# The inverse of 128x128 triangular matrices on four quarters of the array, with sides that alternate

## The reference, cut

```python
def _rwkv7_step(S, inp):
    r, w, k, v, a, b = inp
    sa = jnp.einsum('bhvk,bhk->bhv', S, a)
    S = S * w[:, :, None, :] + sa[..., None] * b[:, :, None, :] + v[..., None] * k[:, :, None, :]
    y = jnp.einsum('bhvk,bhk->bhv', S, r)
    return S, y
...
    xs = tuple(jnp.moveaxis(u, 1, 0) for u in (r_h, w_h, k_h, v_h, -kk, kk * i_h))
    s_new, y = lax.scan(_rwkv7_step, s0.astype(jnp.float32), xs)
```

## Time and profile before

| what | value |
|---|---|
| time, median of 3 runs | 4197.47 us (4194.5 to 4198.24) |
| the profiled execution | 4201.06 us, span 4198.9 us, mean granted clock 0.979 |
| PE busy | 4016.0 us, 96% |
| DVE busy | 2009.9 us, 48% |
| ACT busy | 1386.4 us, 33% |
| chain that ended last | PE 86%, DVE 7%, ACT 2%, issue 2%, DMA 2% |
| pair stage, layer 0 | about 119 to 1153 us |
| pair stage, layer 1 | about 2164 to 3252 us |

### The profile page before, as it was taken

One profiled execution on the slowest core, in us unless ns is written; L12 is line 12 of the kernel. 1 busy time (PEld: TensorE's weight loads), 2 busy tenths in 40 slices (PEclk: granted clock), 3 DMA queues, 4 the chain that ended last, 5 costly groups with the idle time before them and its releaser, 6 DMA issues.

```text
span 4198.9 us, 84192 instructions
## 1 busy us (share of the span) xinstructions
PE 4016.0 (96%) x36004; PEld 3557.1 (85%) x36004; DVE 2009.9 (48%) x3207; ACT 1386.4 (33%) x2169; POOL 288.5 (7%) x463
## 2 busy tenths in 40 slices
PE   7999999999999998999989999999999999989998
PEld 6888888988876687999978888989888766879997
DVE  4545554544345545333355455455443555554444
ACT  4333333333322323222243333343333223232222
POOL 1000000000111021000000000000001110100000
PEclk8999999999999999999999999999999999999998
DMA  6222221222455574443332222212224555412222
GB/s 201 65 63 66 71 72 61 67 68 72 136 201 192 175 231 124 123 134 103 120 108 68 60 69 70 69 62 68 65 77 136 190 194 184 152 48 71 71 76 70
DMA packets 476463, 446.08 MB, mean 106 GB/s; under 512 B 18767, under 2 KB 408969, under 8 KB 475217
## 3 DMA queue, kind: packets, MB, share of 16 engines
q1 hardware_dynamic: 417136, 251.74, 19.8%
q0 software_dynamic: 41568, 155.70, 11.5%
q10 hardware_dynamic: 17408, 33.56, 2.2%
HBM read 344.48 MB, written 96.45 MB: 105 GB/s over the span
## 4 chain that ended last, share of the span: by engine, by line
PE 86%; DVE 7%; ACT 2%; issue 2%; DMA 2%; DVEq 0%; ACTq 0%; SPq 0%; POOL 0%
PE ps L773 84%; DVE scr L2023 4%; PE ps L777 3%; ACT scr L1464 1%; DVE w_lo L2036 1%; DVE h_lo L2023 1%; DMA scr<-in_ada_w_dram 1%; DVE lw L2023 1%; ACT w_hi L1477 0%; DVE scr L2025 0%; DVE acc L2023 0%; DMA w_raw<-in_w_branch_b_dram 0%; DMA scr<-in_x_sample_dram 0%; ACT scr L1617 0%; DMA w_raw<-in_w_ffn_down_dram 0%
## 5 line engine op out<-in xcount | busy, mean ns | idle before, releaser
L773 PE MATMUL ps<-h_hi,w_hi 128*128 128x320 f32 x4544 | 1105.2, 325 | 69.9 <-DVEq L2031 23.9
L773 PE MATMUL ps<-h_lo,w_hi 128*128 128x320 f32 x4544 | 1042.3, 311 | 0.0
L773 PE MATMUL ps<-h_hi,w_lo 128*128 128x320 f32 x4544 | 1041.3, 311 | 0.0
L773 PEld LDWEIGHTS ps<-h_hi,w_hi 128*128 128x128 f32 x4544 | 748.6, 190 | 157.7 <-issue 127.0
L773 PEld LDWEIGHTS ps<-h_lo,w_hi 128*128 128x128 f32 x4544 | 766.8, 190 | 0.0
L773 PEld LDWEIGHTS ps<-h_hi,w_lo 128*128 128x128 f32 x4544 | 766.3, 189 | 0.0
L773 PE MATMUL ps<-scr 64*64 64x64 f32 (+10 forms) x13248 | 732.6, 251 | 13.4 <-DVEq L2187 11.3
L773 PEld LDWEIGHTS ps<-scr 64*64 64x64 f32 (+4 forms) x13248 | 516.1, 141 | 209.9 <-issue 168.2
L1477 ACT ACTIVATE w_hi<-w_raw 128x1024 fp32r<-128x1024 f32 (+1 forms) x468 | 410.7, 878 | 689.6 <-PE ps L773 655.6
L2036 DVE TENSOR_TENSOR w_lo<-w_raw,w_hi 128x1024 fp32r<-128x1024 f32 (+1 forms) x468 | 469.4, 1003 | 254.3 <-ACT w_hi L1477 233.9
L1464 ACT ACTIVATE scr<-ps 128x512 f32<-128x512 f32 (+9 forms) x723 | 343.3, 475 | 581.3 <-PE ps L773 395.3
(11 more groups left out here) (155 smaller groups left out, 3020.5 us busy)
## 6 DMA issues: line engine op xcount, KB each, us to landing
w_raw<-in_w_in_dram SPq DMA_DIRECT2D x180, 512.0 KB, 3.8
scr<-in_ada_w_dram POOLq DMA_DIRECT2D x40, 1024.0 KB, 6.3
scratch_z<-scr SPq DMA_DIRECT2D x124, 320.0 KB, 2.2
scr<-in_state_ret_dram POOLq DMA_DIRECT2D x64, 512.0 KB, 4.7
out_dram<-scr ACTq DMA_DIRECT2D x64, 512.0 KB, 3.0
w_raw<-in_w_ffn_up_dram SPq DMA_DIRECT2D x64, 512.0 KB, 4.1
w_raw<-in_w_ffn_down_dram SPq DMA_DIRECT2D x128, 256.0 KB, 2.7
scr<-scratch_z POOLq DMA_DIRECT2D x24, 1280.0 KB, 8.6
```

Source lines behind the costliest of these rows:

```text
L773: return pe.matmul(out, lhsT, rhs, start=start, stop=stop, skip_group_check=True)
```

## The change

The side on which T1, and the transpose of X with it, stand is now chosen by matrix and level (`turned`): it depends on the group and, at even levels, on which half of the group the matrix is in. The transposed product writes to the side that the next level reads (`crossing`), so `XX` and `T1` change sides between levels. `level_units` sorts the products of a burst into those that stay on their side and those that cross; each kind has a bank (2 and 3) and the burst takes one of each kind in turn. Level 6 of group 1 uses the other half of the partitions. The lt transposes of groups 0 and 1 alternate, those of group 1 crosswise, and DVE's first product of group 1 changes sides back, in two halves. Group 2 stays as it was, in bank 4. On ACT and DVE each group is now emptied by pieces (`group_units`): one access where its products stand in one bank or at equal places of two, two accesses where they don't. ACT takes x and the transposes apart. The waits for groups 0 and 1 of a burst are both for its end (mark .1), but at level 6.

```diff
+        def turned(m, lv):
+            g, other = m // 4, (m // 2) % 2
+            return 0 if g == 2 or lv == LEVELS - 1 else (g + other * (lv - 1)) % 2
+        def side_of(m, d, lv):
+            return half((d + turned(m, lv)) % 2)
+        def crossing(what, m, lv):
+            return (turned(m, lv) + turned(m, lv + 1)) % 2 if what == "xt" else turned(m, lv)
+        def level_units(what, lv):
+            units = [(w, m) for w in (("t",) if what == "T" else ("x", "xt")) for m in range(8)]
+            return [[u for u in units if crossing(*u, lv) == c] for c in range(2)]
+        def unit_at(w, m, lv):
+            for c, units in enumerate(level_units("T" if w == "t" else "X", lv)):
+                if (w, m) in units:
+                    return 2 + c, 64 * units.index((w, m))
+        def group_units(w, g, lv):
+            (b0, at0), (b1, at1) = unit_at(w, 4 * g, lv), unit_at(w, 4 * g + 2, lv)
+            if b0 == b1:
+                return [(slice(4 * g, 4 * g + 4), ps[:, b0, at0:at0 + 256].rearrange("p (t n) -> p t n", n=64))]
+            if b0 < b1 and at0 == at1:
+                return [(slice(4 * g, 4 * g + 4), ps[:, 2:4, at0:at0 + 128].rearrange("p b (t n) -> p b t n", n=64))]
+            return [(slice(4 * g + 2 * i, 4 * g + 2 * i + 2), ps[:, b, at_:at_ + 128].rearrange("p (t n) -> p t n", n=64))
+                    for i, (b, at_) in enumerate(((b0, at0), (b1, at1)))]
...
@@ tensor @@
-                for g in range(3):
+                for g in range(2):
                     W("ve_tr", f"e{g}")
-                    for m in group_blocks(g):
+                for i in range(4):
+                    for g in range(2):
+                        m = 4 * g + i
                         for d in range(2):
-                            last = mm(ps[half(d), 2 + g, 64 * (m % 4):64 * (m % 4) + 64], LTI[half(d), m, half(d)], ident[half(d), half(d)])
-                    M(last, "pe_in", f"lt{g}")
+                            last = mm(ps[side_of(m, d, 1), 2 + g, 64 * i:64 * i + 64], LTI[half(d), m, half(d)], ident[half(d), half(d)])
+                        if i == 3:
+                            M(last, "pe_in", f"lt{g}")
...
+                    if w == "t":
+                        return mm(ps[mine, bank, at_:at_ + 64], LTI[half(d), m, half(d)], XX[half(d), m, 0:64])
+                    if w == "x":
+                        return mm(ps[half(d), bank, at_:at_ + 64], XX[mine, m, 64:128], T1[mine, m])
+                    return mm(ps[side_of(m, d, lv + 1), bank, at_:at_ + 64], T1[mine, m], XX[mine, m, 64:128])
...
+                    for four_ in zip(*level_units(what, lv)):
+                        for w, m in four_:
+                            for d in range(1 if w == "x" and lv == LEVELS - 2 else 2):
+                                ends[m // 4] = product(w, m, d, lv)
+                    for g in range(2):
+                        M(ends[g], "pe_in", f"{what}{lv}.{g}")
...
@@ level 6: T6, then X6 @@
-                            for m in group_blocks(g):
-                                last = mm(ps[64:128, 2 + g, 64 * (m % 4):64 * (m % 4) + 64], LTI[0:64, m, 64:128], XX[0:64, m, 0:64])
-                            M(last, "pe_in", f"T{lv}.{g}")
+                        for i in range(4):
+                            for g in rw_groups(lv):
+                                m = 4 * g + i
+                                last = mm(ps[half(1 - g), 2 + g, 64 * i:64 * i + 64], LTI[0:64, m, 64:128], XX[0:64, m, 0:64])
...
+                                m, mine = 4 * g + i, half(1 - g)
+                                last = mm(ps[0:64, 2 + g, 64 * i:64 * i + 64], T1[mine, m], XTF[mine, m, 64:128])
...
@@ scalar @@
-                        W("pe_in", f"X{lv}.{min(g, 1)}")
+                        W("pe_in", f"X{lv}.{g if lv == LEVELS - 1 else 1}")
...
+                        elif lv == LEVELS - 2:
+                            (_, x_), (_, xt_) = group_units("x", g, lv)[0], group_units("xt", g, lv)[0]
+                            do(XX[0:64, ms, 0:64], x_[0:64])
+                            for d in range(2):
+                                do(XTF[half(d), ms, half(d)], xt_[half(d)])
+                            if g:
+                                do(XTF[0:64, ms, 64:128], xt_[64:128])
                         else:
-                            do(XX[:, ms].rearrange("p t (w n) -> p t w n", w=2), src)
+                            for w, at_ in (("x", 0), ("xt", 64)):
+                                for m_, src in group_units(w, g, lv):
+                                    do(like(XX[:, m_, at_:at_ + 64], src), src)
...
@@ vector @@
-                    tt(XX[:, ms, 0:64], ps[:, 2 + g, 0:64 * k].rearrange("p (t n) -> p t n", n=64),
-                       c1[:, None, C_LC:C_LC + 64].to_broadcast([128, k, 64]), MUL_)
+                    src = ps[:, 2 + g, 0:64 * k].rearrange("p (t n) -> p t n", n=64)
+                    for mine, its in ((half(0), half(1)), (half(1), half(0))) if g == 1 else ((slice(0, 128), slice(0, 128)),):
+                        tt(XX[mine, ms, 0:64], src[its], c1[its, None, C_LC:C_LC + 64].to_broadcast([its.stop - its.start, k, 64]), MUL_)
...
+                                for m_, src in group_units("t", g, lv):
+                                    if len(src.shape) == 4:
+                                        tt(like(T1[:, m_], src), src, mask[:, :, None, :].to_broadcast([128, 2, 2, 64]), MUL_)
+                                    else:
+                                        tt(T1[:, m_], src, mask.to_broadcast([128, src.shape[1], 64]), MUL_)
```

More of the change, by code:

```diff
@@ L467, in block_of, with like @@
             return slice(128 * b, 128 * b + 128)
[L469 to L477, removed]
+        def turned(m, lv):
[20 more added lines that the diff above has]
+                    for i, (b, at_) in enumerate(((b0, at0), (b1, at1)))]
+        def like(a, b):
+            return a.rearrange("p (b t) n -> p b t n", b=2) if len(b.shape) == 4 else a
+        last_products = ps[:, 4, 0:256].rearrange("p (t w n) -> p t w n", w=2, n=64)
         def two_banks(b):
@@ L1028, in rwkv @@
+                W("ve_tr", "e2")
+                for m in group_blocks(2):
+                    for d in range(2):
+                        last = mm(ps[half(d), 4, 64 * (m % 4):64 * (m % 4) + 64], LTI[half(d), m, half(d)], ident[half(d), half(d)])
+                M(last, "pe_in", "lt2")
                 point("lt")
                 next(side, None)
-                def product_t(m, d):
-                    to = slice(64 * (m % 4), 64 * (m % 4) + 64)
-                    return mm(ps[side_of(m, d), 2 + m // 4, to], LTI[half(d), m, half(d)], XX[half(d), m, 0:64])
@@ L1035, in product_x @@
[L1035 to L1044, removed]
@@ L1046, in in_fours, with product @@
-                def in_fours(lv, what, products):
-                    ends = {}
[L1049 to L1054, removed]
+                def product(w, m, d, lv):
+                    if m >= 8:
+                        bank, at_ = 4, 64 * (m % 4) if w == "t" else 128 * (m % 4) + 64 * (w == "xt")
+                    else:
+                        bank, at_ = unit_at(w, m, lv)
+                    mine = side_of(m, d, lv)
+                    if w == "t":
[3 more added lines that the diff above has]
+                    return mm(ps[side_of(m, d, lv + 1), bank, at_:at_ + 64], T1[mine, m], XX[mine, m, 64:128])
@@ L1056, in rwkv, with in_fours @@
+                def in_fours(lv, what):
+                    ends = {}
+                    for four_ in zip(*level_units(what, lv)):
[4 more added lines that the diff above has]
+                        M(ends[g], "pe_in", f"{what}{lv}.{g}")
                 for lv in range(1, LEVELS):
@@ L1073, in rwkv @@
                                     for d in range(2):
-                                        last = product_t(m, d)
+                                        last = product("t", m, d, lv)
                                 M(last, "pe_in", f"T{lv}.2")
@@ L1080, in rwkv @@
                             W("ve_in", f"T{lv}.{g}")
-                            for m in group_blocks(g):
-                                last = mm(ps[0:64, 2 + g, 64 * (m % 4):64 * (m % 4) + 64], T1[64:128, m], XTF[64:128, m, 64:128])
-                            M(last, "pe_in", f"X{lv}.{g}")
+                        for i in range(4):
+                            for g in rw_groups(lv):
+                                m, mine = 4 * g + i, half(1 - g)
+                                last = mm(ps[0:64, 2 + g, 64 * i:64 * i + 64], T1[mine, m], XTF[mine, m, 64:128])
+                                if i == 3:
+                                    M(last, "pe_in", f"X{lv}.{g}")
                     else:
@@ L1090, in rwkv @@
                                 for d in range(2 if lv < S_LEVELS - 1 else 0):
[L1091 removed]
+                                    product("x", m, d, lv)
                                 for d in range(2):
```

(2 more changed lines are left out.)

32 lines of the change are left out of this document (18 added, 14 removed).

## The result

| | before | after |
|---|---|---|
| median of the runs on one chip (5 and 5) | 4194.5 us | 4172.0 us (4165.89 to 4173.1) |
| ratio after to before, 95% interval | | 0.9943 (0.9929 to 0.9958) |
| profiled execution | 4201.06 | 4165.89 |
| span of it | 4198.9 | 4164.1 |

What follows compares the result with a forecast made beforehand. TensorE, busy for 96% of the span, was taken to bound the kernel; gains and losses by place summed to -26.9 us, from 4197.47 to 4170.6 us, with an 80% range of 4158 to 4193.

Steps and rivals of the forecast that it cites:

- X2: Burst X2 up to T3: ScalarE's evictions leave 0.86 or 0.87 us, so only part of the gain; -4.6 us.
- X6: Burst X6: -0.46 us in 12 pairs, nothing in four where PE waits for the filler's bank; -5.5 us.
- Price of a round: PE's small matmul bursts last as long as their fullest quarter, 0.058 us a round; uncovered saving 59 us.
- rival 1: At X1 to X4 PE is not fed instructions fast enough, so these gain nothing: -6.3 us, 4191; 11%.
- Evictions: ScalarE empties PSUM in more pieces, 0.384 us per 128x256, 0.277 per 128x128: +0.40 at X1 and X3, +0.60 at X2 and X4.
- rival 2: At X1 to X4 each cut eviction piece costs a whole one's 0.597 us: sum +10.7, 4208, slower; 6%.
- lt: Ahead of T1: shorter transposes gain nothing, DVE's cut product brings T1 0.45 us later in all pairs; +7.2 us.
- X4: Burst X4 up to T5: ScalarE's longer evictions make a new wait of PE before T5; +2.7 us.
- X1: Burst X1 up to T2: 2.4 us are left, 0.40 + 0.46 needed, so full gain; -7.4 us.
- X5: Burst X5 up to T6: -0.46 us in eight pairs, -0.16 in six where ScalarE is busy; sum -5.5 us.
- Rival 4: Growing waits of PE (T1 by 0.9 us, T5 by as much) let the clock drop: slower; 3%.

Runs made afterwards that it cites:

- experiments 10 to 12: The kernel before profiled once more, unchanged, then the changed kernel twice more, unchanged: 4200.6, 4169.5 and 4170.8 us.
- experiment 1: Changed kernel with the lt transposes all on the diagonal quarters and group 1's first product whole, as before: median 4164.6 us, ratio to before 0.9928.
- 2 and 3: Changed kernel with VectorE's masks of all three groups ahead of its wait: 4142.3 us, ratio 0.9878; the same with lt as before: 4147.3 us.
- experiments 4 and 7: Masks ahead of VectorE's wait plus ScalarE's high part behind X4: 4135.6 us, ratio 0.9861; changed kernel, ScalarE's group 0 pieces at X4 run twice: +11.9 us there.
- experiment 6: Changed kernel with ScalarE's two pieces of group 0 at X1 executed twice (one execution): X1 to T2 changed by 0.00 in every pair.
- Experiment 5: Changed kernel with TensorE waiting at T3 for the eviction of group 2 of X2 too (one execution): X2 to T3 +3.4 us in sum.
- experiment 8: Changed kernel with level 6 as before (T6 and X6 in one quarter each, no seventh X5 piece): median 4182.6 us, ratio 0.9974.
- experiment 9: Changed kernel with X bursts issuing all products of one kind, then all of the other, not in turn: one execution, 4224.1 us.

## Why the prediction was right, point by point

**The total.** That 24 us fit 26.9 is in part luck. The places give 28.6, because X2 gained 2.9 more than forecast and X6 0.7 less; then some 5 us came off again between the places and the whole kernel, which the forecast had not priced: some 2 are the clock's (experiments 10 to 12), the rest is open.

**Price of a round.** Right: 59 us forecast without cover, 59.2 measured as busy time. PE was fed fast enough: X2 shows 80 matmuls in 1.61, so rival 1 is out. The Trainium skill (TensorE: Matmul & The Clock Gate, section on 56 ns against 53.3) states a floor of some 25 ns from start to start. It doesn't hold here: 80 starts in 1.61 us are 20 ns each, and T1's 32 in 0.69 are 22, each with the last one's length counted in.

**Evictions.** Right: a 128x256 piece takes 0.385, also from two banks. Over layer 0's pairs, busy us and mean ns:

```profile
L1504 ACT ACTIVATE scr<-ps 128x256 f32<-128x256 f32 x144 | 55.4, 385 | 15.3 <-PE ps L807 6.4
...
L1504 ACT ACTIVATE scr<-ps 128x128 f32<-128x128 f32 x56 | 15.6, 278 | 26.3 <-PE ps L803 23.3
```

The earlier trace rows had 384 and 277; rival 2 is out.

**lt.** Right in size and sign, shown by experiment 1; that DVE's order and not its speed is the cause is shown by 2 and 3.

**X4.** Right in mechanism and size (+3.0 for +2.7), shown by experiments 4 and 7. The Trainium skill (TensorEngine Tiling, section PSUM Bottleneck) says that tiling doesn't speed up the emptying of PSUM, which may become the bottleneck. The traces agree here (T5 waits 0.81 for ACT) and at T1, where it is VectorE's product that empties PSUM. They don't at X1, where 0.8 us more of it cost nothing (experiment 6), nor at X2, where the prediction saw it too: T3 starts without a wait.

**X2.** The step whose wait was wrong. "It ends at 412.32, T3 is at 413.37": that end is group 2's eviction. PE waits for it only behind the 32 matmuls of groups 0 and 1. The evictions of these two end 0.5 earlier, at 411.81, and the margin was that much wider. Measured -7.5 for -4.6. Experiment 5 puts the wait where I had it, and 3.4 of the 7.5 are lost again.

**X5.** Right in the sum, with one of two waits named (experiment 8).

**X6.** 0.7 us off: in the last pair of a layer the filler waits for its bank once the burst is short (-0.05 and -0.10 instead of -0.46). The margin at this place was not worked out.

**Rival 4**, at 3% and with no price: as written, with the change slower for it, it is out. But the clock does fall in the changed kernel, in two of three profiles, and the forecast put nothing for it. It fell in one of two of the kernel before as well. In these five profiles it took back some 2 us of the gain (2.7 less 0.8).

## What to carry to other kernels

Price a shorter burst by its rounds, then ask at each place which engine is late next, and for which part of the burst: a wait that stands behind half of the matmuls has their time as margin. An edit that shortens the bottleneck engine ahead of a wait is worth nothing until the chain behind that wait is cut, and reordering work that the other engine does while it is idle (here six masks) gave as much as the whole change. Products for different quarters of the array should stand in turn in the program: here that alone was worth 0.77 us a burst.

## What was not expected of the hardware

- With the quarters filled one kind after the other, about three rounds of 0.058 us at the change of kind still overlap: 13 rounds more and not 16 (experiment 9).
- The same waits, of 1.3 to 2.5 us, in the same program let the granted clock fall to 1.2 GHz in one execution and not in another, at 1.0 to 2.4 us each, while everything else between the bursts repeats within 0.01 us. That the waits are the cause is not shown.
